# Attention probabilities copied by DMA before TensorE transposes them, three of four units as float32r

## What is computed

```
hn = rms_norm(x, norm_attn);  proj = hn @ w_in
A: 8 query heads, 2 key/value heads, head size 64; rms norm and rotary positions on q and k
   oa = softmax(q k^T / sqrt(64)) v
B: 8 latent heads: q from a 256-wide latent (64 + 32 rotary), k and v from a 128-wide latent
   ob = softmax(q k^T / sqrt(96)) v
x = x + concat(rms_norm(oa), rms_norm(ob)) @ w_o
h = rms_norm(x, norm_ffn);  x = x + expert_choice_moe(h)   (16 experts, hidden size 1024)
```

## Time and profile before

| | |
|---|---|
| runs shown | 1083.49, 1083.92, 1086.82 us; median 1083.92 |
| profiled execution | 1086.1 us, span of its core 1083.7 us |
| mean granted TensorE clock | 0.986 of full speed |
| TensorE busy | 1044.8 us, 96% of the span |
| DVE busy | 886.0 us, 82% |
| ACT busy | 775.3 us, 72% |
| POOL busy | 423.3 us, 39% |
| transposes of probabilities (L1194) | 512 |
| attention, about 150 to 385 us of the span | 32 heads |

### The profile page before, as it was taken

The page is one execution under the profiler, slowest core; times in us unless marked ns, Lnnn a source line. Parts: engine busy times, 40 slices in busy tenths (PEclk is TensorE's granted clock), DMA queues, the critical chain, the costliest instruction groups (busy, mean ns, idle before and its releaser), DMA issues.

```text
span 1083.7 us, 16970 instructions
## 1 busy us (share of the span) xinstructions
PE 1044.8 (96%) x5689; PEld 896.7 (83%) x5689; DVE 886.0 (82%) x1147; ACT 775.3 (72%) x1095; POOL 423.3 (39%) x394
## 2 busy tenths in 40 slices
PE   8999999999999999998699999999999999999995
PEld 7999978999889987887578888888888888888884
DVE  6787669989999843338899999999999999999991
ACT  7655569888998843344577877877878878788771
POOL 2466576111358502334524432344323444234101
PEclk9999999999999999999799999999999999999998
DMA  8232050010211348741799999999999999999982
GB/s 305 79 116 102 1 197 1 2 41 20 98 41 40 98 109 263 225 164 79 235 417 378 398 400 400 400 421 400 401 400 400 413 408 401 400 400 406 415 310 39
DMA packets 77936, 266.05 MB, mean 245 GB/s; under 512 B 11249, under 2 KB 13516, under 8 KB 77628
## 3 DMA queue, kind: packets, MB, share of 16 engines
q1 hardware_dynamic: 69776, 239.68, 56.9%
q0 software_dynamic: 8048, 25.68, 8.3%
q10 hardware_dynamic: 60, 0.01, 0.0%
HBM read 239.07 MB, written 26.28 MB: 245 GB/s over the span
## 4 chain that ended last, share of the span: by engine, by line
PE 48%; DVE 2%; DMA 1%; issue 1%; ACT 0%; POOLq 0%; POOL 0%; DVEq 0%; ACTq 0%
PE ps L2003 10%; PE ps L2005 10%; PE ps L2004 10%; PE ps L2017 5%; PE ps L2019 5%; PE ps L2018 5%; PE ps L1980 1%; DMA xe<-h,idxT 1%; DMA out<-y,give 1%; DVE lo L2171 0%; DVE idx L1776 0%; DVE affT L1785 0%; DVE gates L1771 0%; ACT hi L2093 0%; POOLq L2274 0%
## 5 line engine op out<-in xcount | busy, mean ns | idle before, releaser
L2171 DVE TENSOR_TENSOR lo<-raw,hi 128x2048 fp32r<-128x2048 f32 x191 | 430.0, 2285 | 32.3 <-ACT hi L2093 32.0
L2093 ACT ACTIVATE hi<-raw 128x2048 fp32r<-128x2048 f32 x192 | 364.6, 1918 | 70.0 <-PE ps L2005 57.3
L2003 PE MATMUL ps<-hi,xehi 128*128 128x512 f32 x480 | 188.3, 392 | 1.3 <-DVE h L2193 1.0
L2005 PE MATMUL ps<-hi,xelo 128*128 128x512 f32 x480 | 186.9, 389 | 0.0
L2004 PE MATMUL ps<-lo,xehi 128*128 128x512 f32 x480 | 186.8, 389 | 0.0
L1939 POOL DMA_INDIRECT xe<-h,take x60 | 111.1, 1851 | 25.1 <-issue 13.7
L2003 PEld LDWEIGHTS ps<-hi,xehi 128*128 128x128 f32 x480 | 90.1, 188 | 20.2 <-issue 1.4
L2005 PEld LDWEIGHTS ps<-hi,xelo 128*128 128x128 f32 x480 | 90.1, 188 | 18.8
L2004 PEld LDWEIGHTS ps<-lo,xehi 128*128 128x128 f32 x480 | 90.2, 188 | 18.1
L1934 POOL COPY take<-idx 128x4 uint32 (+1 forms) x15 | 29.0, 1930 | 193.7 <-DVE xt L2187 187.4
L1361 DVE TENSOR_TENSOR probTlo<-ps,probThi 128x512 fp32r<-128x512 f32 x128 | 87.8, 686 | 12.1 <-ACT probThi L1318 10.0
(11 more groups left out here) (302 smaller groups left out, 2192.3 us busy)
## 6 DMA issues: line engine op xcount, KB each, us to landing
raw<-in_w_down SPq DMA_DIRECT2D x64, 1024.0 KB, 10.0
raw<-in_w_gate SPq DMA_DIRECT2D x60, 1024.0 KB, 9.7
raw<-in_w_up SPq DMA_DIRECT2D x60, 1024.0 KB, 9.3
w_raw<-in_w_in SPq DMA_DIRECT2D x8, 592.0 KB, 9.0
x<-in_x SPq DMA_DIRECT2D x8, 512.0 KB, 3.7
woraw<-in_w_o SPq DMA_DIRECT2D x4, 1024.0 KB, 5.1
o<-attention_out SPq DMA_DIRECT2D x8, 512.0 KB, 4.4
xr<-in_x SPq DMA_DIRECT2D x8, 512.0 KB, 7.0
```

The source lines that it names most:

```text
L2003: pe.matmul(ps[:, dst[n], :], rowhi[:, c, :], hi[w][:, cols], start=c == 0, stop=False)
L2005: last = pe.matmul(ps[:, dst[n], :], rowlo[:, c, :], hi[w][:, cols], start=False, stop=c == KD - 1)
L2093: act.activation(hi[s][:], raw[s][:], ACT.Copy).then_inc(hi_done, 1)
L2171: dve.tensor_tensor(lo[s][:], raw[s][:], hi[s][:].bitcast(F32), ALU.subtract).then_inc(lo_done, 1)
```

## The change

The probabilities get three more buffers, `turn0` to `turn2`, in SBUF. `turn1` and `turn2` take the room of the router's weights, which move to another place. Behind each `exp`, SP copies the 128 x 512 probabilities (256 KB, 2 KB for each partition) from `prob` to `turn` by DMA: `copy_probs`, 128 transfers more. It waits for the `exp` of the unit and for the transposes of the unit three before. TensorE transposes from `turn`, when the copy has landed, and `exp` waits for the copy of unit v-3 in place of its transposes.

The transposes come one step later (unit `u-4` in step `u`), and with them all that follows them: ACT's high part, DVE's low part, values (now in odd steps), outputs. Of the four units of a head, unit 0 is still transposed as float32, interleaved with the products with `halves`. Units 1, 2 and 3 are transposed as float32r: those of unit 2 in a row, those of units 1 and 3 one each ahead of the four low value products. The identity is written as float32r.

SP's stores, `w_o` loads and `route_first` now have places between the copies, given by the copy's number.

```diff
-    STEPS = 8
+    STEPS = 9
+    turn = att["turn"]
+    turn_loaded = project_signals["w_loaded"][0:len(turn)]
+    def loaded(v):
+        return turn_loaded[v % 3], 16 * (v // 3 + 2)
...
-        for h0, h1 in O_PARTS:
-            store_heads(0, h0, h1)
-        sp.wait_ge(o_stored, 16 * len(O_PARTS))
-        for i in range(KD // 2):
+        def load_output_weights(i):
             if i >= 2:
                 sp.wait_ge(wo_lo, 2 * (i - 1))
             sp.dma_start(wo["raw"][:, 2 * (i % 2):2 * (i % 2) + 2, :],
                          a["w_o"].rearrange("(k p) n -> p k n", p=P)[:, 2 * i:2 * i + 2, :]).then_inc(wo_loaded, 16)
-        route_first(sp)
-        for h0, h1 in O_PARTS[:-1]:
-            store_heads(1, h0, h1)
+        def copy_probs(v):
+            sp.wait_ge(exp_done, v + 1)
+            if v >= 3:
+                sp.wait_ge(pt_ready, v - 2)
+            sp.dma_start(turn[v % 3][:], att["p"][v % 3][:]).then_inc(turn_loaded[v % 3], 16)
+
+        for v in range(NU):
+            copy_probs(v)
+            for s, unit in ((0, 0), (1, NU // 2)):
+                for h0, h1 in O_PARTS:
+                    if v == unit + TS * h1 + 10 and v < NU - 1:
+                        store_heads(s, h0, h1)
+            if v == NU // 2 + 13:
+                sp.wait_ge(o_stored, 16 * len(O_PARTS))
+                load_output_weights(0)
+                load_output_weights(1)
+            elif v == NU // 2 + 24:
+                load_output_weights(2)
+            elif v == NU // 2 + 38:
+                load_output_weights(3)
+            elif v == NU - 8:
+                route_first(sp)
...
         def transpose_prob(u, i):
             if i == 0:
-                pe.wait_ge(exp_done, u + 1)
+                pe.wait_ge(*loaded(u))
...
-            turned = pe.transpose(ps[:, T_BANKS[u % 2], cols], att["p"][u % 3][:, cols], k["ident"][:])
+            as_type = F32 if u % TS == 0 else F32R
+            turned = pe.transpose(ps[:, T_BANKS[u % 2], cols].bitcast(as_type), turn[u % 3][:, cols].bitcast(as_type),
+                                  k["ident"][:].bitcast(as_type))
...
                 else:
+                    if between is not None:
+                        transpose_prob(between, i)
                     pe.matmul(ps[0:VD, OT_BANK, cols], v[:, i, 0, :], ptlo[m % 2][:, i, :], start=False, stop=False)
...
-            pair = (u - 6) // 2 if u >= 6 and u % 2 == 0 and (u - 6) // 2 < PAIRS else None
-            turned = u - 3 if 0 <= u - 3 < NU else None
-            output = (u - 11) // TS if u >= 11 and (u - 11) % TS == 0 else None
+            pair = (u - 7) // 2 if u >= 7 and u % 2 == 1 and (u - 7) // 2 < PAIRS else None
+            turned = u - 4 if 0 <= u - 4 < NU else None
+            output = (u - 12) // TS if u >= 12 and (u - 12) % TS == 0 else None
...
                 if v >= 3:
-                    act.wait_ge(pt_ready, v - 2)
+                    act.wait_ge(*loaded(v - 3))
```

More of the change, by code:

```diff
@@ L252, in build @@
         att["ot"] = bm("ot", [P, SEQ])
+        att["turn"] = [bm("turn0", [P, SEQ])]
         assert bm.at <= w_in_end, (bm.at, w_in_end)
@@ L262, in build @@
         wo["small"] = om("smallo", [P, 128])
-        wo["wr"] = om("wr", [P, KD, EXPERTS])
         wo["aff"] = [om(f"aff{i}", [P, 64]) for i in range(2)]
+        att["turn"] += [om(f"turn{i}", [P, SEQ]) for i in (1, 2)]
         assert om.at <= end
@@ L280, in build @@
         wo["gffn"] = om3("gffn", [P, D])
+        wo["wr"] = om3("wr", [P, KD, EXPERTS])
         assert om3.at <= weights_at, (om3.at - weights_at)
@@ L474, in gpsimd_program @@
         steps.wait()
-        pool.affine_select(out=k["ident"][:], in_=k["ident"][:], compare_op=ALU.not_equal, fill=1.0,
+        pool.affine_select(out=k["ident"][:].bitcast(F32R), in_=k["ident"][:], compare_op=ALU.not_equal, fill=1.0,
                            base=0, pattern=[[-1, P]], channel_multiplier=1).then_inc(ident_ready, 1)
@@ L1193, in transpose_prob, with values @@
             cols = slice(i * P, (i + 1) * P)
-            turned = pe.transpose(ps[:, T_BANKS[u % 2], cols], att["p"][u % 3][:, cols], k["ident"][:])
+            as_type = F32 if u % TS == 0 else F32R
+            turned = pe.transpose(ps[:, T_BANKS[u % 2], cols].bitcast(as_type), turn[u % 3][:, cols].bitcast(as_type),
+                                  k["ident"][:].bitcast(as_type))
             if i == TS - 1:
                 turned.then_inc(pt_ready, 1)
-        def values(m):
+        def values(m, between):
             g, qi = units[2 * m]
@@ L1239, in tensor_program @@
                 scores(u)
-            pair = (u - 6) // 2 if u >= 6 and u % 2 == 0 and (u - 6) // 2 < PAIRS else None
-            turned = u - 3 if 0 <= u - 3 < NU else None
-            output = (u - 11) // TS if u >= 11 and (u - 11) % TS == 0 else None
-            for i in range(TS):
-                if output is not None:
-                    turn_output(output, i)
-                if turned is not None:
-                    transpose_prob(turned, i)
-            if pair is not None:
-                values(pair)
+            pair = (u - 7) // 2 if u >= 7 and u % 2 == 1 and (u - 7) // 2 < PAIRS else None
+            turned = u - 4 if 0 <= u - 4 < NU else None
+            output = (u - 12) // TS if u >= 12 and (u - 12) % TS == 0 else None
+            if pair is not None:
+                values(pair, turned)
+            else:
+                for i in range(TS):
+                    if output is not None:
+                        turn_output(output, i)
+                    if turned is not None:
+                        transpose_prob(turned, i)
             if u == NU - 3:
@@ L1253, in tensor_program @@
                 o_transposes(0, 1)
-            elif u == NU + 3:
+            elif u == NU + 4:
                 product(0, 0)
                 product(0, 1)
-            elif u == NU + 4:
+            elif u == NU + 5:
                 product(0, 2)
@@ L1295, in scalar_program @@
         for u in range(NU + STEPS):
-            if u >= 9 and (u - 9) % TS == 0:
-                g = (u - 9) // TS
+            if u >= 10 and (u - 10) % TS == 0:
+                g = (u - 10) // TS
                 act.wait_ge(pv_done, TS // 2 * (g + 1))
@@ L1312, in scalar_program @@
                 keys_values(T - 1)
-            if 0 <= u - 3 < NU:
-                v = u - 3
+            if 0 <= u - 4 < NU:
+                v = u - 4
                 act.wait_ge(pt_ready, v + 1)
@@ L1356, in vector_program @@
         for u in range(NU + STEPS):
-            if 0 <= u - 4 < NU:
-                v = u - 4
+            if 0 <= u - 5 < NU:
+                v = u - 5
                 dve.wait_ge(pthi_done, v + 1)
@@ L1368, in vector_program @@
                 prepare(kind, g)
-            if u >= 11 and (u - 11) % TS == 0:
-                g = (u - 11) // TS
+            if u >= 12 and (u - 12) % TS == 0:
+                g = (u - 12) // TS
                 h = g % HEADS
```

3 lines of the change are left out of this document (2 added, 1 removed).

## The result

| | before | changed |
|---|---|---|
| median us (lowest to highest, runs) | 1083.92 (1083.35 to 1086.82, 5) | 1091.71 (1090.35 to 1093.88, 5) |
| profiled execution, its span | 1086.1, 1083.7 | 1093.88, 1092.0 |
| mean granted TensorE clock | 0.986 | 0.980 |

The ratio is 1.0070, with a 95% interval of 1.0052 to 1.0089: slower by 7.8 us, against a forecast of no change (1084.0, range 1079 to 1092). The range held the time, near its upper end, and slower had been given a chance of 0.33. The sum's own bounds, 1080 to 1088, did not hold it.

A forecast was written before the change was run, and what follows sets the result against it. TensorE was taken to set the pace in MLA heads, with DVE nearly full in GQA heads. Terms −5.6 − 2.8 + 3.7 + 0.9 + 2.5 + 0.7 + 0.7 summed to +0.1, so 1084.0 us on the median, range 1079 to 1092.

The forecast's parts named there:

- start, with the clock: First transposes, whose copy 0 waits behind kv_rowsB on SP's queue: +3.7, plus 0.9 for a lower clock after the idle.
- w_o, first two loads: Two 1 MB loads between copies 77 and 78 delay unit 78's transposes: +2.5, bounds 0 and 3.2.
- load 2: Third w_o load, ahead of copy 89: SP hardly waits for POOL's split; taken 0, up to 1.5.
- `route_first`: Its row loads stand behind copy 120, so copy 121 lands 7.65 later: +0.7, bounds 0 and 2.
- behind attention: What follows attention begins only with its last outputs, so every microsecond of attention passes to the end one for one.
- The pair and its place: Units 1 and 3: transpose plus low product cost 0.181 instead of 0.225, covering each other's loads; 0.35 us per head.
- The row of four: Unit 2 of each head: four float32r transposes in a row take 0.110 each, bounds 0.066 and 0.116; gain 0.
- Rows in float32r are fast too: Rival, unit 2 of each head: transposes fall from 0.110 to 0.066, 0.18 per head, giving 1079.8; chance 0.20.
- The copy itself: Each 256 KB SBUF-to-SBUF copy lands after 2.15, bounds 1.4 and 2.8, within a place of 3.4; steady-state price 0.
- SP is held by POOL: Rival, `route_first` behind copy 120: SP waits for POOL's late w_o splits, issuing no copies; held for 5, 1088; chance 0.05.
- A transpose in float32r costs what it does in float32: Rival, eight pairs per head: transposes still take 0.110, the −8.4 is gone and waits remain, 1092.4; chance 0.12.
- The copy is slow: Rival, ring of copy, transposes and next copy over three units: at 4.5 per copy, +16 in GQA, about 1100; chance 0.05.

The follow-up runs named there:

- e3_rows: The changed kernel with the float32r transposes of units 1 and 3 four in a row ahead of the value products, not between them; 1101.2 us, ratio 1.0129.
- e1_f32: The changed kernel with all transposes in float32 again, at the same places and from the same copies; 1102.5 us, ratio 1.0155.
- e5_spaced: The changed kernel with kv_rowsB, w_o and the first row loads cut up and spread between copies on SP's queue; 1091.8 us, ratio 1.0065.
- e12_rows: e5_spaced with only the later rows of w_o moved, to behind copies 89, 91, 98 and 100; median 1083.2 us, ratio 1.000.

## Why the prediction was right and wrong

The forecast was a gain of 8.4 and losses of 8.5; the trace has a gain of some 9.4 and losses of some 19 in attention, of which some 2 come back behind it. By the steps of the prediction:

| term | forecast | measured (ruler) |
|---|---|---|
| MLA heads | −5.6 | −6.6 (62.7 to 59.4 us per eight) |
| GQA heads | −2.8 | some −2.8 (−1.2 for the seven from unit 4 to 32) |
| start, with the clock | +4.6 | +5.7 |
| w_o, first two loads | +2.5 | +5.5 (unit 77 to 84, with the clock; 84 is at 7.0) |
| load 2 | 0, up to 1.5 | +1.1 |
| load 3 and store | 0 | +1.1 |
| `route_first` | +0.7, up to 2 | +3.8 |
| last copy | +0.7 | +1.6 (last `exp` to last value product) |
| behind attention | 0 | −2.1 (10.4 at the last value product, 8.3 in the span) |

The ruler stood at 0.4 at unit 0 and at 8.8 at unit 127. Some 0.6 of the 10.4 is in no term.

- **The pair and its place** were right: 0.18, and the gain in GQA heads about half, though no row had stood behind that half. Of the 0.17 per pair, e3_rows shows 0.11 to hang on the place: the short load of the low product is covered by the transpose, as the prediction had it.
- **The row of four** was mis-sized: 0.09 per transpose by its loads, not 0.110, so some 0.08 us per head came on top (0.60 for 0.68). That is the 1 us by which the MLA heads gain more. By its starts alone the row is at 0.075 per transpose (0.30 / 4), close to the 0.07 that the prediction had named as a sign of being wrong; part of its cost falls on the product behind it. The prediction had read 0.09 for an uncovered float32r load (254.29) and set it aside for the 0.110 of float32. The rival *Rows in float32r are fast too* had the direction, but 0.066 is not reached. The Trainium skill, TensorE: Matmul & The Clock Gate, section LDWEIGHTS, gives columns / 1.2 in nanoseconds, 107 for such a load. The trace has 0.09 between the starts of float32r loads, and the measurement decides. By the Trainium skill, same page, section Weight-path perf modes, a load of 128 weights of a type other than FP32 is some two times faster. No float32r load here is.
- **The copy itself** was right, 2.2 to 2.3 for 2.15, and hidden in the heads: e1_f32 runs them at the old pace with all copies in place.
- **The step that failed is the price of a copy behind bulk transfers.** I took each bulk transfer at the landing time that it had without copies and added 0.65. Three things were left out. The bulk transfers become slower while copies are in flight (12.5 for 11.0, 8.3 for 7.0). The clock falls after each of the three long waits (5.67, 4.73 and 1.85 us), not only after the first: the 4.2 us at 0.50 at w_o are 2.1 us of TensorE's work. And the issues themselves take time: at w_o exp of unit 77 ends at 292.70 in the changed kernel, the loads are issued at 293.32 and 293.96, and copy 78, which I had put 7.65 behind that exp, lands 10.2 behind it.
- **`route_first`** was priced right in its transfers: copy 121 landed 7.1 us after the first row load was issued, for 7.65. What failed is that SP was free to issue it: POOL's last split of w_o ended 13.7 us later than before (377.94 for 364.26) and held SP for 1.1 of the 1.85 us that TensorE then waited. The rest, 0.75, is the forecast's 0.7. Behind the wait the clock was lower again (0.58 in a window from 385.1 to 389.1), 4.0 × 0.42 = 1.7 us more. The prediction had this as the rival *SP is held by POOL*, at 0.05, but put the clock at nothing there. Whether it would have fallen after a wait of 0.75, no run shows.
- **Behind attention** the forecast passed every microsecond on. Attention lost 10.4 and the kernel 8.3, because the kernel before happened to lose some 2 us at its next row load that the changed one didn't lose. That is luck.
- **The rivals.** 1092.4, the price of *A transpose in float32r costs what it does in float32*, was nearly the time measured, by a mechanism that the trace excludes. A match of times alone would have misled: e1_f32 shows that case, and with the stalls it is 1102.5. The upper end of the range, 1092, lies beyond the sum's own bounds (1088) and near this rival's price; that it held the time is luck as well. *The copy is slow* did not come: 2.2 to 2.3 where nothing large was near.

## What to carry to other kernels

A transfer put between two engines of a tight pipeline is hidden only while it lands within its place (here some 3 to 5 us; behind bulk transfers it took up to 8.9): list every bulk transfer of the stage, and price the small one by what is in flight with it, in any queue, plus the clock that TensorE loses behind the wait. Cutting bulk transfers up helps, but each piece has its own deadline with a third engine (here POOL's splits), and a queue that waits for that engine holds everything behind it. Where a loss of this kind meets a true gain, measure each alone: here the gain was some 8 to 10 us and the copies cost 16.

## What the hardware showed that was not expected

- A float32r transpose of 128 x 128 costs 0.09 us in a row (its load) and 0.06 between products with 64-column weights (its columns); a float32 one costs 0.11 in either place. The float32 price is therefore not that of loading 128 columns alone, as I had read it; which part of it is float32's own, no run shows.
- A second queue does not shield a transfer: 9.3 us for 256 KB, though issued first, against 2.2 alone.
- 256 KB from SBUF to SBUF land after 2.2 to 2.3 us (minimum and median of every kernel with copies); where nothing large is near they can still take 4.8.
- Two kernels with the same program up to that point differ by 1.5 us there, by whether the clock fell after a short wait (e5_spaced and e12_rows, units 80 to 84).
